# Two weight units taken together at block starts, and a result's squares summed partly on TensorE, in a two-block transformer kernel

## The reference

```
# first block, once
h = h + rmsnorm(mixed @ w_out, norm_mix_post)            # mixed: conv and sparse attention of rmsnorm(h)
hn = rmsnorm(h, norm_x_pre)                              # cross attention to mem (256 x 1024)
kx, vx = split(rmsnorm(mem, norm_mem) @ w_kv_x)
h = h + rmsnorm(softmax(q(hn) kx) vx @ w_o_x, norm_x_post)
g, up = split(rmsnorm(h, norm_ffn_pre) @ w_gate_up)      # d_ff = 2816
h = h + rmsnorm((silu(g) * up) @ w_down, norm_ffn_post)
# second kind, layers 0 and 1: no norm on a result
x = x + (sigmoid(ga) * attention + sigmoid(gb) * conv) @ w_out
x = x + (silu(g) * up) @ w_down                          # g, up of rmsnorm(x)
```

## Time and profile before

| | us |
|---|---|
| runs | 2424.97, 2427.34, 2428.83 |
| median | 2427.34 |
| profiled execution | 2428.8 |
| its span, first to last instruction | 2426.7 |
| PE, DVE, ACT, POOL busy | 2316.5, 1282.6, 922.9, 194.8 |
| mean granted clock of PE | 0.977 of full |

### The profile page before, as it was taken

One profiled execution on the slowest core, in us unless ns is written; L12 is line 12 of the kernel. 1 busy time (PEld: TensorE's weight loads), 2 busy tenths in 40 slices (PEclk: granted clock), 3 DMA queues, 4 the chain that ended last, 5 costly groups with the idle time before them and its releaser, 6 DMA issues.

```text
span 2426.7 us, 30171 instructions
## 1 busy us (share of the span) xinstructions
PE 2316.5 (95%) x11144; PEld 1850.4 (76%) x11144; DVE 1282.6 (53%) x1844; ACT 922.9 (38%) x1541; POOL 194.8 (8%) x143
## 2 busy tenths in 40 slices
PE   7999998997999997999998999999999998999999
PEld 5877688885888885886666888888887666888887
DVE  6456547325444324798665444432798665444433
ACT  4533444234332223222873333222332873332322
POOL 2000021012000002001012000001001002000001
PEclk9999799998999998999999999999999999999999
DMA  5211013211322221321112222232321012222231
GB/s 195 104 69 36 36 53 139 87 38 50 106 101 99 93 103 46 121 87 53 36 53 87 87 87 104 94 114 81 122 87 53 36 53 87 80 93 104 87 108 66
DMA packets 29200, 202.22 MB, mean 83 GB/s; under 512 B 3232, under 2 KB 3872, under 8 KB 5408
## 3 DMA queue, kind: packets, MB, share of 16 engines
q1 hardware_dynamic: 27072, 195.05, 22.6%
q10 hardware_dynamic: 2016, 5.71, 0.6%
HBM read 198.64 MB, written 2.10 MB: 83 GB/s over the span
## 4 chain that ended last, share of the span: by engine, by line
PE 85%; DVE 6%; issue 4%; ACT 3%; POOL 0%; DMA 0%; ACTq 0%; DVEq 0%; POOLq 0%
PE bank L338 24%; PE bank L340 24%; PE bank L339 24%; PE bank L759 2%; PE bank L786 1%; ACT w_hi L259 1%; PE bank L1738 1%; PE bank L1712 1%; DVE cy L1960 1%; DVE h L1393 1%; PE bank L1725 1%; PE bank L775 1%; DVE x_lo L329 1%; PE bank L1339 1%; PE bank L288 1%
## 5 line engine op out<-in xcount | busy, mean ns | idle before, releaser
L338 PE MATMUL bank<-x_hi,w_hi 128*128 128x512 f32 x2080 | 835.6, 402 | 54.6 <-DVE x_lo L329 30.2
L340 PE MATMUL bank<-x_hi,w_lo 128*128 128x512 f32 x2080 | 817.7, 393 | 0.0
L339 PE MATMUL bank<-x_lo,w_hi 128*128 128x512 f32 x2080 | 817.7, 393 | 0.0
L263 DVE TENSOR_TENSOR w_lo<-w_raw,w_hi 128x2048 fp32r<-128x2048 f32 x168 | 387.4, 2307 | 386.7 <-ACT w_hi L259 386.7
L338 PEld LDWEIGHTS bank<-x_hi,w_hi 128*128 128x128 f32 x2080 | 395.5, 190 | 146.4 <-DVE x_lo L329 32.5
L259 ACT ACTIVATE w_hi<-w_raw 128x2048 fp32r<-128x2048 f32 x168 | 321.1, 1914 | 378.0 <-PE bank L340 376.1
L340 PEld LDWEIGHTS bank<-x_hi,w_lo 128*128 128x128 f32 x2080 | 395.2, 190 | 84.8
L339 PEld LDWEIGHTS bank<-x_lo,w_hi 128*128 128x128 f32 x2080 | 395.8, 190 | 81.2 <-issue 2.9
L340 PE MATMUL bank<-f_hi,w_lo 128*128 128x512 f32 x528 | 208.6, 395 | 0.0
L338 PE MATMUL bank<-f_hi,w_hi 128*128 128x512 f32 x528 | 208.6, 395 | 0.0
L339 PE MATMUL bank<-f_lo,w_hi 128*128 128x512 f32 x528 | 208.5, 395 | 0.0
(11 more groups left out here) (306 smaller groups left out, 2457.9 us busy)
## 6 DMA issues: line engine op xcount, KB each, us to landing
w_raw<-w_d SPq DMA_DIRECT2D x184, 1024.0 KB, 4.8
h<-x_d ACTq DMA_DIRECT2D x4, 512.0 KB, 7.8
out_d<-h SPq DMA_DIRECT2D x4, 512.0 KB, 4.9
tab<-rope_d ACTq DMA_DIRECT2D x2, 640.0 KB, 4.0
memT<-mem_d ACTq DMA_DIRECT2D x1, 1024.0 KB, 5.5
stage<-cmask_d ACTq DMA_DIRECT2D x1, 384.0 KB, 8.5
pos_i<-pos_d ACTq DMA_DIRECT2D x1, 256.0 KB, 8.7
gains<-pack_d ACTq DMA_DIRECT2D x1, 228.5 KB, 6.0
```

The source lines that it names most:

```text
L263: dve.tensor_tensor(w_lo[:, u.slot, :], w_raw[:, u.slot, :], w_hi[:, u.slot, :], ALU.subtract).then_inc(lo_ready, 1)
L338: pe.matmul(dst, wh[:, k, cols], hi[:, kx_, 0:width], start=start, stop=False)
L339: pe.matmul(dst, wh[:, k, cols], lo[:, kx_, 0:width], start=False, stop=False)
L340: return pe.matmul(dst, wl[:, k, cols], hi[:, kx_, 0:width], start=False, stop=stop)
```

## The change

- `linear_joined` takes the place of `linear_start` at five starts (`U_QX`, the three FFNs, the layers): of two units each k is taken by both before the next k; both must be split beforehand. The columns and rows of the norm move to the third unit: columns ahead of it, rows after four k of its first half. In the layers the second unit runs two k behind the first and waits (`free`) for `h_ready`, since its banks held the last results. For this the second unit is split ahead of the block's start: one split more is done in the part before last of the down products.
- In the first block a result's two squares come ahead of its copies. POOL adds six tiles (`sum_result_squares`), and PE sums the last two straight from the square buffers into the same columns (`result_columns`, with `picks`, whose columns place each block's sum).
- After `U_OX` and `U_DN` (`near`): the root's table is loaded ahead (`root_table`), the last pair's copies come behind the root and behind the row copy, and the split that stood there moves: for `U_OX` behind the fourth tile of the next norm on ACT and behind the last on DVE.
- In the FFN the split of the unit three ahead comes first on ACT and after the two scalings on DVE; PE now waits for `f_lo_done` of the tile whose banks it takes.
- SP loads one dummy unit more at the end.

```diff
+        def sum_result_squares(pool, n):
+            for k in range(1, 6):
+                pool.wait_ge(sq_ready, n * 8 + k + 1)
+                pool.wait_ge(acc_ready if k > 1 else stat_done, n * 7 + k - 1 if k > 1 else n)
+                pool.tensor_tensor(acc[:, :], sq[:, 0, :] if k == 1 else acc[:, :], sq[:, k % 2, :],
+                                   ALU.add).then_inc(acc_ready, 3 if k == 5 else 1)
...
+        def result_columns(pe, n):
+            pe.wait_ge(acc_ready, n * 7 + 7)
+            pe.wait_ge(std_ready, n)
+            for i, src in enumerate((acc[:, :], sq[:, 0, :], sq[:, 1, :])):
+                if i:
+                    pe.wait_ge(sq_ready, n * 8 + 6 + i)
+                for b_ in range(QB):
+                    mm = pe.matmul(bank[:, AUX, 0:QB], src[:, b_ * P:(b_ + 1) * P], picks[:, QB * b_:QB * b_ + QB],
+                                   start=(i + b_ == 0), stop=(i + b_ == QB + 1))
+            mm.then_inc(stat_done, 1)
...
+        def linear_joined(pe, us, chunk_ready, norm, lag=0, free=None):
+            def chunk(u, k):
+                for m in range(2):
+                    mm = products(pe, u, m, k, k, u.slot, k == 0, k == 7, x_hi, x_lo)
+                if k == 7:
+                    mm.then_inc(unit_done, 1)
+
+            for u in us[:2]:
+                pe.wait_ge(lo_ready, u.n + 1)
+            for k in range(8 + lag):
+                if k < 8:
+                    chunk_ready(k)
+                    chunk(us[0], k)
+                if k == lag and free is not None:
+                    free()
+                if k >= lag:
+                    chunk(us[1], k - lag)
+            u = us[2]
+            pe.wait_ge(lo_ready, u.n + 1)
+            stat_columns(pe, norm)
+            for m in range(2):
+                for k in range(8):
+                    mm = products(pe, u, m, k, k, u.slot, k == 0, k == 7, x_hi, x_lo)
+                    if (m, k) == (0, 4):
+                        stat_rows(pe, norm)
+            mm.then_inc(unit_done, 1)
...
@@ ffn_up_act
+                split_hi(act, Unit(u.n0 + SLOTS, layer, i))
                 act.wait_ge(gu_scaled, n * 2 + 1)
                 act.activation(silu[:, :], g, ACT.Silu).then_inc(silu_done, 1)
                 act.wait_ge(f_ready, n + 1)
                 act.activation(pick(f_hi, j, i), up, ACT.Copy).then_inc(f_hi_done, 1)
-                split_hi(act, Unit(u.n0 + SLOTS, layer, i))
@@ ffn_up_dve
                 dve.tensor_tensor(up, up, rbc[:, :], ALU.mult).then_inc(gu_scaled, 1)
+                split_lo(dve, Unit(u.n0 + SLOTS, layer, i))
...
-                split_lo(dve, Unit(u.n0 + SLOTS, layer, i))
@@ ffn_pe
+            def body(u, j, i):
+                pe.wait_ge(f_lo_done, tile_of(j, i) + call * FT + 1)
+                linear(pe, u)
+            units(pe, first + 3, FT - 3, layer, body)
...
-                            pe.wait_ge(f_lo_done, call * FT + min(8 * part + 8, FT))
+                            pe.wait_ge(f_lo_done, call * FT + (FT if part == 2 else FT - 2))
@@ cross_pe, after the first unit of U_KV
-                    stat_columns(pe, NORM_MIXP)
+                    result_columns(pe, NORM_MIXP)
@@ ends of U_OX and U_DN
+        def root_table(act):
+            act.activation(jcol[:, 0:1], eps_c[:, 0:1], ACT.Sqrt)
...
+        def last_rows(act, n, y, src):
+            std_columns(act, n)
+            out_copy(act, y, 6, src[0])
+            take_rows(act, n)
+            out_copy(act, y, 7, src[1])
...
             for k in range(DT):
                 act.wait_ge(h_ready, 8 + k + 1)
                 pre_norm_hi(act, 2, NORM_F, k, "ffn_pre")
+                if k == 3:
+                    split_hi(act, Unit(U_OX + 6))
@@ layer_pe
+            linear_joined(pe, [Unit(base + s, L) for s in range(3)], lambda k: pe.wait_ge(pre_lo, pre * 8 + k + 1), norm,
+                          2, lambda: pe.wait_ge(h_ready, L * 24 + 16))
@@ layer_act (layer_dve alike)
-            for s in (1, 2):
-                split_hi(act, Unit(base + s, L))
+            split_hi(act, Unit(base + 2, L))
...
-                    if g < 3 or part == 0:
+                    if g < 3 or part < 2:
                         split_hi(act, Unit(base + V_DN + 3 * g + part + 3, L))
```

More of the change, by code:

```diff
@@ L434, in body @@
                 dve.tensor_tensor(pick(f_lo, j, i), up, pick(f_hi, j, i), ALU.subtract).then_inc(f_lo_done, 1)
-                split_lo(dve, Unit(u.n0 + SLOTS, layer, i))
             units(dve, first, FT, layer, body)
         def ffn_pe(pe, first, pre, norm, call, layer):
[L440 to L443, removed]
+            linear_joined(pe, [Unit(first + s, layer) for s in range(3)],
+                          lambda k: pe.wait_ge(pre_lo, pre * 8 + k + 1), norm)
+            def body(u, j, i):
+                pe.wait_ge(f_lo_done, tile_of(j, i) + call * FT + 1)
+                linear(pe, u)
+            units(pe, first + 3, FT - 3, layer, body)
             down = first + FT
@@ L1302, in cross_pe @@
                 tokens_major(pe, u, m_hi, m_lo, range(2), 0, 2 * P, lambda b_: (2 * u.slot + b_, 0)).then_inc(unit_done, 1)
[L1303 to L1304 removed]
+            linear_joined(pe, [Unit(U_QX + s) for s in range(3)], lambda k: pe.wait_ge(pre_lo, 8 + k + 1), NORM_X)
+            for j in range(3, 4):
                 linear(pe, Unit(U_QX + j))
@@ L1363, in cross_pe, with out_squares, out_copy, out_evac_act @@
                 linear(pe, Unit(U_OX + j))
-            stat_columns(pe, NORM_XP)
+            result_columns(pe, NORM_XP)
             stat_rows(pe, NORM_XP)
             ffn_pe(pe, U_GU, 2, NORM_F, 0, None)
-            stat_columns(pe, NORM_FP)
+            result_columns(pe, NORM_FP)
             stat_rows(pe, NORM_FP)
-        def out_evac_act(act, first, n, y):
+        def root_table(act):
+            act.activation(jcol[:, 0:1], eps_c[:, 0:1], ACT.Sqrt)
+        def out_squares(act, n, g, src):
+            for m in range(2):
+                square(act, n, 2 * g + m, src[m])
+        def out_copy(act, y, k, src):
+            act.activation(y[:, k, :], src, ACT.Copy).then_inc(y_ready, 1)
+        def last_rows(act, n, y, src):
[3 more added lines that the diff above has]
+            out_copy(act, y, 7, src[1])
+        def out_evac_act(act, first, n, y, near):
             for j in range(4):
@@ L1374, in out_evac_act @@
                 act.wait_ge(unit_done, u.n + 1)
[L1375 to L1379, removed]
-                split_hi(act, Unit(u.n0 + 3))
+                src = [bank[:, 2 * u.slot + m, :] for m in range(2)]
+                out_squares(act, n, j, src)
+                if j < 3 or not near:
+                    for m in range(2):
+                        out_copy(act, y, 2 * j + m, src[m])
+                    split_hi(act, Unit(u.n0 + 3))
+                if j == 2 and near:
+                    root_table(act)
+            if near:
+                last_rows(act, n, y, src)
         def post_norm_dve(dve, q, n, y, gain, pre, pre_gain, between=lambda k: None):
@@ L1465, in cross_act @@
                     if part == 2:
-                        for m in range(2):
-                            k, src = 2 * g + m, bank[:, 2 * (g % 2) + m, :]
-                            act.activation(y_ffn[:, k, :], src, ACT.Copy).then_inc(y_ready, 1)
-                            square(act, NORM_FP, k, src)
-                    if g < 3 or part == 0:
+                        src = [bank[:, 2 * (g % 2) + m, :] for m in range(2)]
+                        out_squares(act, NORM_FP, g, src)
+                        if g < 3:
+                            for m in range(2):
+                                out_copy(act, y_ffn, 2 * g + m, src[m])
+                    if g < 3 or part < 2:
                         split_hi(act, Unit(u.n0 + 3))
-            std_columns(act, NORM_FP)
-            take_rows(act, NORM_FP)
+                    if g == 3 and part == 1:
+                        root_table(act)
+            last_rows(act, NORM_FP, y_ffn, src)
             for k in range(DT):
```

37 lines of the change are left out of this document (21 added, 16 removed).

## The result

| | before | changed |
|---|---|---|
| first comparison, median of 6 runs each | 2427.44 us | 2413.64 us |
| lowest and highest | 2422.90, 2430.51 | 2406.95, 2417.78 |
| ratio, 95% interval | | 0.9942 [0.9922, 0.9962] |
| second comparison, median (14 and 6 runs) | 2428.71 us | 2408.45 us |
| ratio, 95% interval | | 0.9915 [0.9891, 0.9938] |

I had worked out 20.9 us.

What follows compares the result with a forecast made beforehand. PE, busy 95% of the span, bounds the kernel, so only filling its holes counts. 10.5 + 13.5 - 1.9 - 1.2 = 20.9 us gained gives a 2406 us median; forecast's own range 2404 to 2409, 8 in 10 for 2401 to 2414.

Steps and rivals of the forecast that it cites:

- rival 2: Added column groups are slow, 1.87 us each instead of 0.95; 1.8 us less gain at each passage: 2410; chance 0.11.
- first passage: From U_OX's result over two norms to the FFN: joined units out at 581.1 instead of 591.6, gain 10.5 us.
- second passage: From U_DN to layer 0: both joined units out at 968.6 instead of 982.1, gain 13.5 us.
- sum of the attention's output: After U_KV's first unit: two more column groups on PE delay DVE's tiles, 1.9 us lost, bounds 0 to 3.7.
- stall before the FFN's fourth unit: PE's fourth unit waits for the first tile's f_lo: 0.4 us each, 1.2 us lost at three FFNs.
- layer 0's DVE and the start of layer 1: DVE loses 5.4 us of lead in the layers, swallowed by 6.4 us idle: 0; layer 1's joined start: 0.
- Squares and sums: Both passages: squares first, PE sums the last two; sums end at 551.15 instead of 554.32, 3.2 us earlier.
- Join: Two units tile by tile: 12 matmuls per x_lo, 2.72 us against DVE's 2.99; no PE hole over 0.5 us.
- rival 6: Join fills nothing, x_lo coming every 2.99 us and second unit's weights late; only 3.3 us gained: 2424; chance 0.03.
- rival 4: A table switch costs more than its row: twice 1.3 us on each FFN's first tile, 7.8 us: 2414; chance 0.03.
- rival 3: DVE's lead isn't enough: all 5.4 us reach PE in both layers: 2417; chance 0.06.
- Rival 5: The f_lo wait binds every FFN tile, making the kernel slower; at 1 us above two units (21.8 us) 2463; chance 0.02.

Runs made afterwards that it cites:

- experiment 1: The changed kernel run once more with no edit (the "again" of the table); median 2408.45 us, ratio 0.9915 to the kernel before.
- experiment 8: Changed kernel with the attention's output alone summed as before the change, the passages kept as changed; median 2406.02 us (5 runs).
- Experiments 2: Changed kernel with the join undone at all five starts, the split ahead of the second unit kept; median 2417.20 us (9 runs).
- experiment 3: Changed kernel with PE's sum of the last two tiles, squares ahead of copies and the early root table all undone; median 2416.86 us.
- Experiment 5: Changed kernel with the norm's rows sent after the fourth tile instead of the fifth in the FFN; median 2407.92 us.
- experiment 6: Changed kernel with a 1-element Silu at the head of the FFN's loop, one table load a turn instead of two; median 2412.39 us.
- experiment 7: Changed kernel with the Silu table loaded behind the root of the FFN's norm, while ACT waits for the rows; median 2409.25 us.

## Why the prediction was right, and where it was off

The forecast of 2406 us had the mechanism, and most of its terms came out. The time itself fits less well: the first median of 2413.64 lies outside the forecast's own 2404 to 2409 and only 0.4 inside the 2401 to 2414, with three of the six runs above 2416. That the range held is in part luck. The mean of all runs, 2410.8, is the time of rival 2, whose mechanism the traces rule out. The terms compare as follows (negative: lost). The measured ones are from the table of units and the experiments.

| step | worked out | measured |
|---|---|---|
| first passage | 10.5 | 10.0 (changed), 10.4 (again) |
| second passage | 13.5 | 12.9 (changed), 13.7 (again) |
| sum of the attention's output | -1.9 | -0.7 (changed), -1.3 (again); -1.0 to -1.5 by experiment 8 |
| stall before the FFN's fourth unit, three times | -1.2 | -3.9 |
| layer 0's DVE and the start of layer 1 | 0 | -0.9 (changed), -0.2 (again) |
| sum | 20.9 | 17.4 (changed), 18.7 (again) |

- *Squares and sums.* DVE's first tile was put 3.2 us earlier; it is 3.21 in the first passage of the changed kernel. Over the 24 passages of the 12 traces with the new sums it comes 4.5 to 5.3 us after the block's last product, so 2.8 to 3.7 us earlier: 5.3 where half clock began 2.1 us after that product, 4.5 where it began 4.7 us after it (experiment 1, its two passages). The added column groups ran at the pace of 0.95 us for eight that I had taken: sixteen took 1.95 us, up to 2.30 where half clock began among them, not the 3.7 of rival 2. All that hangs on POOL's two adds is gone.
- *Join.* No hole in the first pair, one of 1.27 us in the second at 939.22, where the prediction allowed 0.5 and named such a hole as a sign of being wrong; it hardly lengthened the pair. The third unit begins 29.8 us after DVE's first tile there, where 29.7 were forecast, and 27.2 to 28.4 in the first passage, for 27.6. Experiments 2 and 3 show the two parts to be worth 6.4 to 6.8 us net and 5.0 to 6.7 us, neither of them nothing; rival 6 would have left 3 us in all. What is left, of the second passage above all, I put down to the split ahead; no run shows it alone.
- *The stall was mis-sized, the term that was furthest off: 1.2 us forecast, 3.9 measured.* Its chain was right: I had 7.7 us from DVE's start to f_lo, the trace has 7.64 (586.05 to 593.69). Its start was not. I let DVE start 5.0 us after the column sums, as in the kernel before, where the rows went out after four k; the changed code has the test behind the products of k = 4, so they go out after the fifth, three matmuls later (the text on the change says four as well, wrongly). Experiment 5 moved them back and 0.66 us of 1.30 went. The rest beyond my 0.4 lies in the restart: PE begins 0.14 us after f_lo, and its first matmul takes 0.49 us and not 0.39.
- *The table loads.* Both are there in the first turn, as the earlier trace rows had led me to expect. I added only the first, rightly: experiment 6 shows the second to lie beside w_lo, though its way is only 0.4 us shorter than DVE's. Between a load's end (587.24) and w_hi (587.26) there is no drain, so rival 4 is out; experiment 7 gave back 1.30 us a stall by taking one load out of the way. The Trainium skill (ScalarE: Activation LUTs, What ACT_TABLE_LOAD costs) adds a drain of some 1.38 us to each; this case's traces don't agree.
- *The keys.* I had 1.9 us with nothing to take it back. DVE's tile is 1.65 to 1.8 us later and 1.0 to 1.5 are left at unit 30.
- *Layers.* Layer 0's first twelve units take 173.78 instead of 173.65 us, so the lead of 5.4 us that DVE loses stays swallowed; rival 3 is out. Rival 5 is out too: only three tiles of 66 wait for f_lo.
- *What I did not have.* At the start of layer 1, 8 of the 12 traces with a join show 0.6 to 1.25 us more than the 34.1 us of the kernel before, and 4 show nothing (under 0.15). In all eight PE stands 0.3 to 1.0 us before the layer's first matmul, and the profile names no releaser. The one trace without the join has none. What makes it come and go stays open.
- *The median.* I set the profiled execution 1.5 us above the median and was content. The larger matter was that a kernel's runs differ by 16 us with the clock: the first six runs came out at 2413.64 and the next six at 2408.45, so that the median shown first is 7.6 us above my number, while the means of all runs differ from my gain by 2.8.

## What to carry to other kernels

When a wait is added, place its start in the new code and not in the old: count the instructions ahead of the point from which its chain runs. And when something is to be taken off a chain, first lay all the ways to its next meeting point side by side; 21 loads off the way that lay beside another brought nothing, one ahead of their fork brought 1.3 us each time it was met. Sums moved onto the busiest engine paid only where that engine stood idle: with the moved copies and table they brought DVE's tiles 2.8 to 3.7 us forward in two places, and cost 1.0 to 1.5 us in the third. And compare edits at a like clock only where they leave the clock alone.

## What the runs showed of the hardware

- The mean granted clock explains most of the difference between runs of one kernel: 2.07 us for each 0.001, with 1.8 us left over, in 123 runs. A mean lower by 0.001 is 4.8 us more at half clock in 2400, so one us at half clock costs 0.43 us on average. Dense matmuls of 512 columns would lose 0.47, by their spacing of 0.427 us there and 0.227 at full clock.
- Half clock cost only where PE had work for it. With the hole filled, half clock in a passage fell from 10.2 to 3.4 us and brought 0.5 to 0.6 us in the first passage and 0.3 at most in the second.
- Eight narrow matmuls took 0.95 us behind dense work, whether of one column or of four (547.21), and 1.86 to 1.87 us behind a pause of 3.92 us, at half clock (556.82 in experiment 3). So these pauses cost 0.9 us more than their own length.
